# First chunk's turns in a row, two modulation slots moved, and the last expert by column halves with GpSimd adding the others' sum

## The chip, the cores and the metric

The kernel runs on one core of a Trainium2 chip. The metric is device time in microseconds (us). TensorE (PE) has a row of matmuls and one of weight loads (PEld) in the profile; VectorE is DVE, ScalarE is ACT, GpSimd is POOL, SyncE is SP. Line numbers (L447) are those of the kernel before.

## The reference

`reference` runs 256 tokens of width 1024 through two blocks of two layers each, all in float32. Block 1: a gMLP layer (`gelu(rmsnorm(h) @ w_in)`, its second half normed and mixed over 128 tokens by `w_s`, times the first half, `@ w_out`), a gated MLP with a causal convolution of width 3 (`conv_ffn`, hidden 2816), then keys and values, chunked attention with a relative bias, and a second `conv_ffn`. Block 2 is steered by a vector `c`: `silu(c) @ ada_w + b` gives shift, scale and gate for each half layer. Its even layer has forgetting and sliding window attention and a gated MLP, its odd layer sparse attention and a mixture of 8 experts, two for each token:

```
for e in experts:            # tokens that chose e
    y_e = (silu(x @ w_gate[e]) * (x @ w_up[e])) @ w_down[e]
x = x + gate * sum_e(weight_e * y_e)
out = rms_norm(x, final_norm)
```

## The kernel before

**Weights as a stream.** All weights come in one row of slots of up to 128 x 2048 numbers (1 MB), in the order of use (`Plan`, L101 to 163). SP's `load` (L359) fills a ring of `RAW` = 6 buffers; slot s waits until slot s - 6 is used. For precision each weight slot is split in two: ACT writes `whi`, the rounded part (`split`, L1122), DVE writes `wlo`, the rest (`split`, L1665, its instruction L1677). PE makes three products for each 128 rows (`mm3`, L446: lines L447 to L449), high by high, high by low and low by high. The activations are held as `xhi` and `xlo` (`ahi`, `alo` for hidden values). A weight slot of four 128-row blocks costs PE 24 matmuls of 512 columns where there are two token tiles, 12 where there is one gathered tile (the experts).

**Chunks.** A projection is worked in chunks of 512 columns (`product`, L453): two slots each where the input is 1024 wide, six for 2816 (`down0`, `down1`: the first of the six is half a slot). Below, the slots of one projection are numbered from 0. `gmlp_in` has chunks 0 to 3, chunk 0 in slots of 2, 2 and 4 blocks (`FIRST`).

**Modulation slots.** The weights of `c` (48 slots of 4 x 512 columns, 24 for each layer) stand between the others, behind the slots that `Plan` names with `behind`. DVE multiplies such a slot by `silu(c)` right after its split of the slot before it (`modulate`, L1685: four instructions, L1701 and L1703). After each second one PE sums the columns (`ada_turn`, L655, L663) once it is through the slot in front; DVE takes the sums in (`take_cols`, `ada_cols`) before the next pair.

**Order of the work.** Each engine has its own program, written out by hand, and engines wait for semaphores. DVE splits up to two slots ahead (`AHEAD`), three and more before a change of stage (`LEAD`, `MORE`). In the convolution stage DVE's `convolve` splits the first slots of `down0` between its taps and its product with the gate. `residual_then` (L1909) adds the last two chunks of `down0` to `h`, splits slot 1 of `kv`, and then makes blocks 4 to 7 of the next `xhi` and `xlo` (`tail`, L1759), for which PE's slot 1 of `kv` waits.

**Start.** PE turns (transposes) blocks 0 to 3 of both token tiles of x (L760), then blocks 4, 5 and 6, 7 (`two`, L539) as the two turning banks come free. ACT copies each pair with the norm's gain (`tail`), DVE casts it to `xhi` and takes the rest for `xlo`. ACT then makes the statistics (`stats`: sums of squares, roots), and only after them splits slots 3 and 4; DVE computes the rope's angles (L2084 to L2097) and then splits slots 3 and 4 (`skip`). Three small loads are issued first on ACT's queue (`posi`, `rows`, `cols`), one from POOL (`rw`).

**Experts.** Expert 0, a hardware loop over 6, and the last one. Each has 12 slots for the hidden values (`hidden` 0 to 5, the last pair half as wide) and 6 for the output (`out_of`, slots o0 to o5, o5 a half). `add_expert` adds the scattered output of the expert before to the sum `macc`, left half while `hidden` 0 is done, right half at j = 4. For the last expert DVE also multiplies `macc` by the gate and adds it to `h` (`sum_into_h`, L2441, tile 0 among the splits of o3 and o4, tile 1 behind them all), and its output is gated, split in high and low, scattered by PE (`scatter(gated=True)`) and added to `h` (`add_gated`, L2429), then normed and stored.

Of the kernel before, what the change touches and what calls it, by code (L numbers as in the profile page):

```python
# [26 lines left out]
P = 128  # L27
# [73 lines left out]
class Plan:  # L101
# [89 lines left out]
def build_program(nc, x_in, cols_in, rows_in, vg_in, fg1_in, fg_in, pos_in, ws_in, toep_in, rw_in, stream_in, out):  # L191
# [3 lines left out]
    with ctx:  # L195
# [120 lines left out]

        def trb(b):

            return ps[:, 6 + b, :].rearrange("p (k s) -> p k s", k=2)
# [36 lines left out]
        def _(sp):  # L356
# [49 lines left out]
        def _(g):  # L406
# [20 lines left out]
            g.dma_start(rw[:, :, :], rw_in.rearrange("(k p) e -> p k e", p=P)).then_inc(sem("rw_landed"), 16)  # L427


# [4 lines left out]
            g.memset(bias[0:DH, :, P + DH:S], NEG).then_inc(sem("bias_ready"), 1)  # L434

            g.wait_ge(sem("h_added"), 7 * NT)
            g.dma_start(gates[:, 0, :], fg_in.to_broadcast([P, D])).then_inc(sem("fg_landed"), 16)


        @block.tensor  # L440
        def _(pe):
# [315 lines left out]
            for t in range(NT):  # L757
                pe.wait_ge(sem(f"x_landed{t}"), 16)
                for k in range(4):
                    m = pe.transpose(trb(k // 2)[:, k % 2, t * P:(t + 1) * P], h[:, t, k * P:(k + 1) * P], ident[:, :])  # L760
# [3 lines left out]
            two(h, 2)  # L764
# [4 lines left out]
            product(W, KT, xhi, xlo, at_slot=blocks_ready, mid=lambda j: None if j else two(h, 3), parts=FIRST)  # L769
# [7 lines left out]
            def spatial(j):  # L777
                if j == 0:
# [3 lines left out]
                    pe.wait_ge(sem("ada_taken"), 1)  # L782
# [209 lines left out]
            def scatter(gated=False):  # L992

                T.up("x_y")
                if not gated:
                    pe.wait_ge(sem("y_copied"), T("x_y"))
                for n in range(2):
                    if gated:
                        pe.wait_ge(sem("yg_split"), T.up("x_ys"))
# [34 lines left out]
            def out_of(i, first=False, turn_next=False):  # L1034
# [3 lines left out]
                for j in range(6):  # L1038
# [13 lines left out]
                    m.then_inc(sem("w_used"), 1)  # L1052


            def expert(i, first=False, last=False):
# [14 lines left out]
                out_of(i, first, turn_next=not last)  # L1070
# [10 lines left out]
            for _ in range(6):  # L1081
                pe.matmul(ps[:, 2, 0:P], tri[:, :], ones[:, :], start=True, stop=True)
            scatter(gated=True)
# [4 lines left out]
            with pe.If(most > P):  # L1088
                with pe.Fori(0, NE) as i:
                    T.loop(i, x_acc=6, x_tr=6, x_g=1, x_xt=2, x_y=1, x_a=6, x_s=2, x_gt=1, x_ys=2)  # L1090
                    n = pe.value_load(count[0:1, bass.ds(i, 1)])
                    with pe.If(n > P):
# [10 lines left out]
                        scatter(gated=True)  # L1103
                    with pe.Else():
                        pe.drain()
                        for name, k in (("g_psum", 2), ("g_turned", 2), ("x_tr", 6), ("gt_psum", 1), ("w_used", EXP), ("y_psum", 2)):
# [5 lines left out]
        def _(act):  # L1112
            T = Tally()
            act.dma_start(posi[:, :], pos_in).then_inc(sem("rows_landed"), 16)
            act.dma_start(rows[:, :], rows_in.to_broadcast([P, R_END])).then_inc(sem("rows_landed"), 16)
# [246 lines left out]
            act.activation(st[:, 26:27], ones[:, 0:1], ACT.Identity)  # L1362
            for t in range(NT):
                act.wait_ge(sem(f"x_landed{t}"), 16)
            act.wait_ge(sem("cols_landed"), 16)
            for r in range(2):
                tail(xT_c, cols[:, C_GA:C_GA + KT], rounds=(r,))
                split(r + 1)
            tail(xT_c, cols[:, C_GA:C_GA + KT], rounds=(2,))
            split(3)  # L1370
            tail(xT_c, cols[:, C_GA:C_GA + KT], rounds=(3,))
            stats(h, False)
# [193 lines left out]
            def output(i, first=False, gated=False):  # L1566
                used[0] += 6
                split(used[0] + MORE, i, EXP)
                if not first:
                    act.wait_ge(sem("y_psum"), T.up("x_y", 2))  # L1570
                if gated:
                    for n in range(2):
                        act.wait_ge(sem("yg"), T.up("x_yg"))
                        act.activation(yhi[:, 4 * n:4 * n + 4, :], yg[:, n * W:(n + 1) * W].rearrange("p (k c) -> p k c", c=P), ACT.Copy)\
                            .then_inc(sem("yg_hi"), 1)
# [37 lines left out]
            with act.If(most > P):  # L1613
                with act.Fori(0, NE) as i:
                    T.loop(i, x_tr=6, x_g=2, x_gp=2, x_y=2, x_sg=6, x_gt=1, x_yg=2)
# [14 lines left out]
                    with act.Else():  # L1630
                        act.drain()
                        for name, k in (("xt_copied", 2), ("xg", 2), ("hi_done", EXP), ("x_silu", 6), ("gt_copied", 1), ("x_hi", 6), ("yg_hi", 2)):
# [17 lines left out]
        def _(dve):  # L1650
# [420 lines left out]

            for r in range(2):
                tail(xT_c, (r,))
                split(r + 1)
            tail(xT_c, (2,))
            split(3)
            tail(xT_c, (3,))
            moments()
            inverses()
            dve.wait_ge(sem("cols_landed"), 16)  # L2080
# [22 lines left out]
            skip(1, slots=len(FIRST))  # L2103
# [7 lines left out]
            take_cols(1)  # L2111
# [297 lines left out]
            def gate_output(i):  # L2409

                dve.wait_ge(sem("w_used"), i * EXP + used[0])
                for n in range(2):
                    c = slice(n * W, (n + 1) * W)
                    dve.tensor_tensor(yg[:, c], ps[:, 3 + n, :], gates[:, 1, c], ALU.mult).then_inc(sem("yg"), 1)
                for n in range(2):
                    dve.wait_ge(sem("yg_hi"), T.up("x_yh"))
                    k = slice(4 * n, 4 * n + 4)
                    dve.tensor_tensor(ylo[:, k, :], yg[:, n * W:(n + 1) * W].rearrange("p (k c) -> p k c", c=P),
                                      yhi[:, k, :].bitcast(F32), ALU.subtract).then_inc(sem("yg_split"), 1)
# [9 lines left out]
            def add_gated(i, name):  # L2429

                for n in range(2):
                    dve.wait_ge(sem("y_psum"), T.up("x_y"))
                    for t in range(NT):
                        o = h[:, t, n * W:(n + 1) * W]
# [5 lines left out]

            def sum_into_h(t):  # L2441

                link(dve.tensor_tensor(macc[:, t, :], macc[:, t, :], gates[:, 1, :], ALU.mult))
                link(dve.tensor_tensor(h[:, t, :], macc[:, t, :], h[:, t, :], ALU.add))

# [5 lines left out]
            def expert(i, first=False, last=False):  # L2451
# [17 lines left out]
                if last:  # L2469
                    sum_into_h(0)  # L2470
# [6 lines left out]
                if last:  # L2477
                    sum_into_h(1)
                    gate_output(i)
# [12 lines left out]
            assert pos[0] == used[0] == QAT["more"]  # L2492

            most = dve.value_load(count[0:1, NE:NE + 1])
            with dve.If(most > P):
                at_last = T("x_y")
                add_gated(slice(NE - 1, NE), "y_added")
                with dve.Fori(0, NE) as i:
                    T.loop(i, x_xg=2, x_silu=6, x_hi=6, x_a=6, x_y=2, x_yh=2, dve=2, xg_ready=2)
# [15 lines left out]
                    with dve.Else():  # L2515
                        dve.drain()
                        for name, k in (("places", 1), ("dve", 2), ("xg_ready", 2), ("g_taken", 1), ("lo_done", EXP), ("x_tok", 6),
                                        ("x_a", 6), ("x_tr_free", 6), ("yg", 2), ("yg_split", 2), ("y_added", 1)):
# [119 lines left out]
```

## Time and profile before

| | us |
|---|---|
| median of 3 runs | 1508.49 (1505.85 to 1509.45) |
| profiled execution, its own time | 1511.99 |
| its span, first to last instruction | 1510.2 |
| PE busy | 1443.1 |
| DVE busy | 1220.9 |
| ACT busy | 899.4 |
| POOL busy | 5.6 |

The span lies 1.8 us below the profiled execution's own time. Busy time of PE contains overlap: matmuls are pipelined, and the start of one to the start of the next is what a matmul costs. A row of the timeline has the start in us, the length in us, engine, line, operation, output <- input, shape and count; in brackets stands the idle time of the engine before it and what ended it. Rows of one kind that follow each other are merged (x2).

### The profile page before, as it was taken

The page shows a single profiled execution, that of the slowest core. Times are in us where ns is not written, and L with a number is a line of the kernel's source. Part 1 is how long each engine was busy: PE and PEld are TensorE (multiplying, and loading weights), DVE is VectorE, ACT ScalarE, POOL GpSimd, SP SyncE. Part 2 cuts the span into 40 slices and gives each one's busy share as a digit, 9 for nine tenths or more (in the row PEclk, how much of TensorE's full clock was granted, in tenths as well). Part 3 has the DMA queues.
Part 4 walks back from the last instruction along what each step waited for, and adds up shares of the span by engine and source line. Part 5 has one row for each costly group of instructions (what it writes and reads, how often), then busy time and mean ns, then how long its engine had stood idle before and what let it go on. Part 6 is the DMA issues. An engine that isn't in the chain of part 4 may idle for free.

```text
span 1510.2 us, 19548 instructions
## 1 busy us (share of the span) xinstructions
PE 1443.1 (96%) x7128; PEld 1185.2 (78%) x7129; DVE 1220.9 (81%) x1664; ACT 899.4 (60%) x1207; POOL 5.6 (0%) x18
## 2 busy tenths in 40 slices
PE   6999999999999999998999999979899999999996
PEld 5888888887788887886788887856687888888885
DVE  6776879767767889878878788696688989999997
ACT  6555664556666563567433334446676877787764
POOL 0000000000000000000000000000000000000000
PEclk9999999999999999999999999979899999999999
DMA  8565446875355458561566786422289899898983
GB/s 295 230 227 191 167 169 235 336 265 221 112 205 186 154 181 305 212 240 59 205 262 256 268 311 231 167 84 85 112 326 343 317 330 325 341 355 328 335 325 138
DMA packets 53422, 356.15 MB, mean 236 GB/s; under 512 B 6096, under 2 KB 7120, under 8 KB 12896
## 3 DMA queue, kind: packets, MB, share of 16 engines
q1 hardware_dynamic: 52592, 352.15, 62.7%
q0 software_dynamic: 320, 2.65, 0.5%
q8 instruction: 49, 0.80, 0.2%
q10 hardware_dynamic: 432, 0.30, 0.1%
q14 instruction: 29, 0.24, 0.1%
HBM read 354.03 MB, written 1.05 MB: 235 GB/s over the span
## 4 chain that ended last, share of the span: by engine, by line
PE 76%; DVE 14%; ACT 5%; DMA 3%; issue 2%; SPq 0%; DVEq 0%; ACTq 0%
PE ps L447 23%; PE ps L449 22%; PE ps L448 22%; DVE wlo L1677 4%; DMA raw<-stream_dram 3%; PE ps L612 1%; ACT whi L1133 1%; DVE acc L1703 1%; PE ps L539 1%; PE ps L663 1%; PE ps L688 1%; DVE tok L1928 1%; ACT attn_scratch L1319 1%; PE ps L717 1%; DVE xlo L1767 1%
## 5 line engine op out<-in xcount | busy, mean ns | idle before, releaser
L1677 DVE TENSOR_TENSOR wlo<-raw,whi 128x2048 fp32r<-128x2048 f32 (+2 forms) x302 | 645.5, 2163 | 91.9 <-ACT whi L1133 78.4
L1133 ACT ACTIVATE whi<-raw 128x2048 fp32r<-128x2048 f32 (+2 forms) x302 | 541.8, 1817 | 183.1 <-DMA raw<-stream_dram 177.8
L447 PE MATMUL ps<-whi,xhi 128*128 128x512 f32 (+3 forms) x1360 | 534.0, 393 | 13.5 <-DVE xlo L2382 4.2
L449 PE MATMUL ps<-whi,xlo 128*128 128x512 f32 (+3 forms) x1360 | 522.6, 384 | 0.0
L448 PE MATMUL ps<-wlo,xhi 128*128 128x512 f32 (+3 forms) x1360 | 521.8, 384 | 0.0
L447 PEld LDWEIGHTS ps<-whi,xhi 128*128 128x128 f32 x1360 | 257.1, 189 | 70.2 <-issue 8.5
L449 PEld LDWEIGHTS ps<-whi,xlo 128*128 128x128 f32 x1360 | 256.9, 189 | 51.6
L448 PEld LDWEIGHTS ps<-wlo,xhi 128*128 128x128 f32 x1360 | 257.5, 189 | 46.7
L447 PE MATMUL ps<-whi,ahi 128*128 128x512 f32 x440 | 174.7, 397 | 3.7 <-DVE wlo L1677 2.5
L449 PE MATMUL ps<-whi,alo 128*128 128x512 f32 x440 | 171.7, 390 | 0.0
L448 PE MATMUL ps<-wlo,ahi 128*128 128x512 f32 x440 | 171.3, 389 | 0.0
L1703 DVE SCALAR_TENSOR_TENSOR acc<-raw,cs,acc 128x512 f32<-128x512 f32 x168 | 126.1, 751 | 5.1
L1928 DVE SCALAR_TENSOR_TENSOR tok<-ps,cols,tok 128x255 f32<-128x255 f32 (+1 forms) x176 | 72.7, 475 | 41.1 <-ACT tok L1283 40.3
L447 PEld LDWEIGHTS ps<-whi,ahi 128*128 128x128 f32 x440 | 82.6, 188 | 23.2 <-issue 4.1
L449 PEld LDWEIGHTS ps<-whi,alo 128*128 128x128 f32 x440 | 82.6, 188 | 17.7
L448 PEld LDWEIGHTS ps<-wlo,ahi 128*128 128x128 f32 x440 | 82.7, 188 | 16.3
L1187 ACT ACTIVATE tok<-ps,st 128x512 f32<-128x512 f32 x64 | 40.5, 685 | 55.1 <-PE ps L612 35.8
L1288 ACT ACTIVATE tok<-tok 128x512 f32<-128x512 f32 x22 | 13.9, 632 | 65.6 <-DVE tok L1928 65.6
L1283 ACT ACTIVATE tok<-ps,cols 128x256 f32<-128x256 f32 x88 | 42.5, 576 | 3.8 <-DVEq L1946 3.8
L1552 ACT ACTIVATE tok<-ps 128x256 f32<-128x256 f32 (+1 forms) x48 | 17.3, 360 | 42.4 <-PE ps L449 42.2
L1319 ACT ACTIVATE attn_scratch<-attn_scratch,sx 128x128 f32<-128x128 f32 x80 | 35.3, 445 | 10.0 <-DVE sx L2009 9.9
L1303 ACT ACTIVATE tok<-ps 128x512 f32<-128x512 f32 x11 | 6.6, 598 | 52.9 <-PE ps L449 52.9
(316 smaller groups left out, 1164.9 us busy)
## 6 DMA issues: line engine op xcount, KB each, us to landing
raw<-stream_dram SPq DMA_DIRECT2D x315, 1024.0 KB, 4.9
raw<-stream_dram SPq DMA_DIRECT2D x32, 512.0 KB, 4.7
attn_scratch<-toep_dram POOLq DMA_DIRECT2D x1, 2048.0 KB, 11.8
raw<-stream_dram SPq DMA_DIRECT2D x2, 528.0 KB, 4.4
h<-x_dram SPq DMA_DIRECT2D x2, 512.0 KB, 4.7
y<-tok SPq DMA_DIRECT2D x4, 256.0 KB, 2.6
head_scratch<-w_s_dram SPq DMA_DIRECT2D x1, 512.0 KB, 14.4
head_scratch<-vg_dram SPq DMA_DIRECT2D x1, 512.0 KB, 11.5
```

What stands on the lines that cost most here:

```text
L447: pe.matmul(o, xh, wh, start=start, stop=False)
L448: pe.matmul(o, xh, wl, start=False, stop=False)
L449: return pe.matmul(o, xl, wh, start=False, stop=stop)
L539: last = pe.transpose(trb(n % 2)[0:src.shape[1], k - r, t * P:(t + 1) * P], src, ident[:, :])
L1133: act.activation(whi[:, q % SPL, 0:w], raw[:, s % RAW, 0:w], ACT.Copy).then_inc(sem("hi_done"), 1)
L1187: m = act.activation(dst[:, t], src[:, t], func, scale=st[:, 6 + t:7 + t])
L1283: m = act.activation(conv[:, f, :], ps[:, 6 + f // 2, (f % 2) * S:(f % 2 + 1) * S], ACT.Identity, scale=sc, bias=bi)
L1319: m = act.activation(x, x, ACT.Exp, bias=neg_max(u, t), scale=-1.0, accum_out=total(u, t))
L1552: act.activation(sgx[:, 0:m], ps[:, (2, 0, 1)[j % 3], m:2 * m], ACT.Silu).then_inc(sem("x_silu"), 1)
L1677: dve.tensor_tensor(low(q)[:, 0:w], raw[:, s % RAW, 0:w], whi[:, q % SPL, 0:w].bitcast(F32), ALU.subtract).then_inc(sem("lo_done"), 1)
L1703: m = dve.scalar_tensor_tensor(acc[:, :], wk, cs[:, kk:kk + 1], acc[:, :], ALU.mult, ALU.add)
L1928: m = dve.scalar_tensor_tensor(o, src, cols[:, c:c + 1], o, ALU.mult, ALU.add)
```

## The change

1. `gmlp_in` has no modulation slots any more; `down0` gets one behind its slot 2 and `kv` one behind its slot 1.
2. PE turns all eight blocks of x in a row into four banks (`first_of`), followed by four matmuls that nobody reads. ACT writes `xhi` out of the banks (`first_high`), DVE `xlo` (`first_low`).
3. ACT splits slot 3 between squares and roots and slots 4 and 5 behind them; DVE splits slots 3, 4 and 5 ahead of the angles.
4. `cols` is loaded first; `posi` and `rows` are issued by ACT once `x` and `cols` have landed; `w_s` is issued behind slot 3, `vg` behind slot 6, `rw` behind the bias load at the second layer.
5. `out_of` of the last expert works o3 to o5 by column halves: the left half of all three, then the right half. The left half is gated and split while PE works on the right one and scattered ahead of o5's right part (`scatter_left`); the right half is scattered unsplit, as float32 (`scatter_right`). The six matmuls in front of the scatter (L1082) are gone.
6. POOL does `sum_into_h`, by column halves, each half as soon as `add_expert` has finished it; DVE waits for it ahead of `add_gated`.

```diff
-        proj("gmlp_in", 2 * D, G_ORDER, layer=0, behind=(4, 5), first=FIRST)
+        proj("gmlp_in", 2 * D, G_ORDER, first=FIRST)
-        proj("down0", D, kt=FK, layer=0, behind=(4, 5, 7, 8, 10, 11))
-        proj("kv", 2 * D, layer=0, behind=(2, 3, 5, 7))
+        proj("down0", D, kt=FK, layer=0, behind=(2, 4, 5, 7, 8, 10, 11))
+        proj("kv", 2 * D, layer=0, behind=(1, 2, 3, 5, 7))
...
+        def first_of(r):
+            return ps[:, (6, 7, 4, 5)[r], :].rearrange("p (k s) -> p k s", k=2)
...
-                if s == 2:
+                if s == 3:
                     sp.dma_start(ws, ...)
-                if s == 3:
+                if s == 6:
                     sp.dma_start(vg, ...)
...
+            for n, added in enumerate(("y_left", "y_added")):
+                c = slice(n * W, (n + 1) * W)
+                g.wait_ge(sem(added), NE - 1)
+                g.tensor_tensor(macc[:, :, c], macc[:, :, c], gates[:, 1, c]..., ALU.mult).then_inc(sem("h_summed"), 1)
+                g.wait_ge(sem("h_summed"), 2 * n + 1)
+                g.tensor_tensor(h[:, :, c], macc[:, :, c], h[:, :, c], ALU.add).then_inc(sem("h_summed"), 1)
...
-                for k in range(4):
-                    m = pe.transpose(trb(k // 2)[:, k % 2, ...], h[:, t, ...], ident[:, :])
+                for k in range(KT):
+                    m = pe.transpose(first_of(k // 2)[:, k % 2, ...], h[:, t, ...], ident[:, :])
-            two(h, 2)
+            for _ in range(4):
+                pe.matmul(ps[:, 2, 0:S], ident[:, :], h[:, 1, 0:S], start=True, stop=True)
...
+            def scatter_left():
+                pe.wait_ge(sem("yg_split"), T.up("x_ys"))
+                for t in range(NT):
+                    pe.matmul(ps[:, 5 + 2 * t, :], GT[:, t, :], yhi[:, 0:4, :], start=True, stop=False)
+                    pe.matmul(ps[:, 5 + 2 * t, :], GT[:, t, :], ylo[:, 0:4, :], start=False, stop=True)...
+            def scatter_right():
+                pe.wait_ge(sem("yg"), 2 * T("x_ys"))
+                for t in range(NT):
+                    pe.matmul(ps[:, 3 + t, :], GT[:, t, :].bitcast(F32), yg[:, W:D], ...)...
...
+                for n in range(2 if by_half < 6 else 0):
+                    for j in range(by_half, 6):
+                        ...
+                        elif j == 5:
+                            scatter_left()
+                        ...
+                    if n == 0:
+                        m.then_inc(sem("y_half"), 1)
...
+            def first_high(r):
+                act.wait_ge(sem("tr"), T.up("tr"))
+                for j in range(2):
+                    k = 2 * r + j
+                    m = act.activation(xhi[:, k, :], first_of(r)[:, j, :], ACT.Identity, scale=cols[...])
+            for r in range(2):
+                first_high(r)
                 split(r + 1)
+            for r in range(2, 4):
+                first_high(r)
             split(3)
-            stats(h, False)
+            act.activation(st[:, 26:27], ones[:, 0:1], ACT.Sqrt)
+            squares(h, False)
+            split(4)
+            roots()
+            split(6)
...
             moments()
+            split(4)
             inverses()
+            skip(1, slots=len(FIRST))
+            split(6)
...
-                    sum_into_h(0)
...
-                    sum_into_h(1)
-                    gate_output(i)
+                    gate_output(i, by_half=True)
...
+            dve.wait_ge(sem("h_summed"), 4)
```

## Rows read from the trace of the kernel before

**Rows 1.** The page: busy time by engine, and the chain's shares by engine.

```profile
PE 1443.1 (96%) x7128; PEld 1185.2 (78%) x7129; DVE 1220.9 (81%) x1664; ACT 899.4 (60%) x1207; POOL 5.6 (0%) x18
...
PE 76%; DVE 14%; ACT 5%; DMA 3%; issue 2%; SPq 0%; DVEq 0%; ACTq 0%
```

**Rows 2.** Timeline of the start, 12 to 53 us: PE, ACT and DVE.

```profile
13.45 0.63 PE L448 MATMUL ps<-wlo,xhi 128*128 128x512 f32 x1
...
13.88 0.63 PE L449 MATMUL ps<-whi,xlo 128*128 128x512 f32 x1
...
16.19 1.91 ACT L1133 ACTIVATE whi<-raw 128x2048 fp32r<-128x2048 f32 x1 [0.80 <-DMA raw<-stream_dram]
...
18.14 2.29 DVE L1677 TENSOR_TENSOR wlo<-raw,whi 128x2048 fp32r<-128x2048 f32 x1 [1.15 <-ACT whi L1133]
...
29.75 0.50 PE L447 MATMUL ps<-whi,xhi 128*128 128x512 f32 x1 [1.60 <-DVE wlo L1677]
...
40.97 1.27 ACT L1187 ACTIVATE tok<-ps,st 128x512 f32<-128x512 f32 x2 [3.59 <-PE ps L449]
...
46.21 0.95 PE L663 MATMUL ps<-ones,acc 128*128 128x1 f32 x8
...
50.46 4.49 DVE L1677 TENSOR_TENSOR wlo<-raw,whi 128x2048 fp32r<-128x2048 f32 x2
...
58.45 3.61 PE L784 MATMUL ps<-tok,head_scratch 128*128 128x256 f32 x16
```

**Rows 3.** Stretches: us, busy time and count of each engine, PEclk, DMA share, GB/s.

```profile
30.00:41.00 11.00, 11.00 (x50) 9.07 (x50) 10.48 (x12) 6.83 (x7) 0.00 (x0) 1.00 0.43 162
...
1081.00:1085.00 4.00, 4.00 (x10) 3.13 (x11) 3.41 (x4) 3.23 (x2) 0.00 (x0) 0.50 0.00 0
```

**Rows 4.** Timeline of DVE and PE at the start of `down0`.

```profile
231.11 2.29 DVE L1677 TENSOR_TENSOR wlo<-raw,whi 128x2048 fp32r<-128x2048 f32 x1
...
243.82 2.33 DVE L1703 SCALAR_TENSOR_TENSOR acc<-raw,cs,acc 128x512 f32<-128x512 f32 x3
...
248.32 2.29 DVE L1677 TENSOR_TENSOR wlo<-raw,whi 128x2048 fp32r<-128x2048 f32 x1
...
250.76 0.47 PE L447 MATMUL ps<-whi,ahi 128*128 128x512 f32 x1 [0.62 <-DVE wlo L1677]
```

**Rows 5.** Timeline of DVE and PE at the start of `kv`.

```profile
290.07 2.29 DVE L1677 TENSOR_TENSOR wlo<-raw,whi 128x2048 fp32r<-128x2048 f32 x1
...
295.81 0.69 DVE L1767 TENSOR_TENSOR xlo<-tok,xhi 128x512 fp32r<-128x512 f32 x1
...
296.55 0.50 PE L447 MATMUL ps<-whi,xhi 128*128 128x512 f32 x1
```

**Rows 6.** Timeline of the last expert: DVE and PE.

```profile
1456.52 2.29 DVE L1677 TENSOR_TENSOR wlo<-raw,whi 128x2048 fp32r<-128x2048 f32 x1 [0.19 <-ACT whi L1133]
...
1462.44 0.48 PE L447 MATMUL ps<-whi,xhi 128*128 128x512 f32 x1
...
1479.15 4.48 DVE L1677 TENSOR_TENSOR wlo<-raw,whi 128x2048 fp32r<-128x2048 f32 x2
...
1486.52 1.22 DVE L2443 TENSOR_TENSOR tok<-tok,gates 128x1024 f32<-128x1024 f32 x1
...
1489.03 2.29 DVE L1677 TENSOR_TENSOR wlo<-raw,whi 128x2048 fp32r<-128x2048 f32 x1
...
1491.47 0.47 PE L447 MATMUL ps<-whi,ahi 128*128 128x512 f32 x1 [0.88 <-DVE wlo L1677]
...
1495.91 1.29 DVE L2414 TENSOR_TENSOR tok<-ps,gates 128x512 f32<-128x512 f32 x2 [0.63 <-PE ps L449]
...
1499.36 2.73 DVE L2435 SCALAR_TENSOR_TENSOR h<-ps,comb,h 128x512 f32<-128x512 f32 x4 [0.70 <-PE ps L1003]
```

**Rows 7.** Timeline of POOL and DVE at 302 us.

```profile
301.58 2.33 DVE L1703 SCALAR_TENSOR_TENSOR acc<-raw,cs,acc 128x512 f32<-128x512 f32 x3
...
302.07 0.95 POOL L434 MEMSET attn_scratch<- 64x1024 f32 x1 [11.29 <-DMA attn_scratch<-toep_dram]
```

More of the change, by code:

```diff
@@ L763, in _ @@
                         T.up("tr")
-            two(h, 2)
+            for _ in range(4):
+                pe.matmul(ps[:, 2, 0:S], ident[:, :], h[:, 1, 0:S], start=True, stop=True)
             def blocks_ready(j, k):
                 pe.wait_ge(sem("x_ready"), T.up("x_ready", FIRST[j] // 2))
-            product(W, KT, xhi, xlo, at_slot=blocks_ready, mid=lambda j: None if j else two(h, 3), parts=FIRST)
+            product(W, KT, xhi, xlo, at_slot=blocks_ready, parts=FIRST)
             pe.wait_ge(sem("ws_landed"), 16)
@@ L1032, in turn, with out_of @@
                 T.up("x_tr")
-            def out_of(i, first=False, turn_next=False):
+            def out_of(i, first=False, turn_next=False, by_half=6):
                 if not first:
                     pe.wait_ge(sem("y_added"), T("x_y"))
-                for j in range(6):
+                for j in range(by_half):
                     if j == 1 and turn_next:
@@ L1069, in expert @@
                     gather()
-                out_of(i, first, turn_next=not last)
+                out_of(i, first, turn_next=not last, by_half=3 if last else 6)
             gather()
@@ L1080, in _ @@
             expert(0, last=True)
-            for _ in range(6):
-                pe.matmul(ps[:, 2, 0:P], tri[:, :], ones[:, :], start=True, stop=True)
-            scatter(gated=True)
+            scatter_right()
             pe.wait_ge(sem("counted"), 1)
@@ L1102, in _ @@
                         out_of(i)
-                        scatter(gated=True)
+                        scatter_left()
+                        scatter_right()
                     with pe.Else():
                         pe.drain()
-                        for name, k in (("g_psum", 2), ("g_turned", 2), ("x_tr", 6), ("gt_psum", 1), ("w_used", EXP), ("y_psum", 2)):
+                        for name, k in (("g_psum", 2), ("g_turned", 2), ("x_tr", 6), ("gt_psum", 1), ("w_used", EXP), ("y_psum", 2 * NT)):
                             pe.sem_inc(sem(name), k)
@@ L1361, in _ @@
             act.wait_ge(sem("pool"), 5)
-            act.activation(st[:, 26:27], ones[:, 0:1], ACT.Identity)
+            act.activation(st[:, 31:32], ones[:, 0:1], ACT.Identity)
             for t in range(NT):
@@ L1568, in output @@
                 split(used[0] + MORE, i, EXP)
-                if not first:
+                if not first and not gated:
                     act.wait_ge(sem("y_psum"), T.up("x_y", 2))
                 if gated:
[L1572 to L1575, printed above, removed]
+                    act.wait_ge(sem("yg"), T.up("x_yg", 2) - 1)
+                    act.activation(yhi[:, 0:4, :], yg[:, 0:W].rearrange("p (k c) -> p k c", c=P), ACT.Copy).then_inc(sem("yg_hi"), 1)
                 else:
@@ L2070, in _, with first_low @@
                 dve.sem_inc(sem(name), 1)
+            def first_low(r):
+                dve.wait_ge(sem("x_high"), r + 1)
+                for j in range(2):
+                    k = 2 * r + j
+                    m = dve.scalar_tensor_tensor(xlo[:, k, :], first_of(r)[:, j, :], cols[:, C_GA + k:C_GA + k + 1],
+                                                 xhi[:, k, :].bitcast(F32), ALU.mult, ALU.subtract)
+                m.then_inc(sem("x_ready"), 1)
+            dve.wait_ge(sem("cols_landed"), 16)
             for r in range(2):
-                tail(xT_c, (r,))
+                first_low(r)
                 split(r + 1)
-            tail(xT_c, (2,))
+            for r in range(2, 4):
+                first_low(r)
             split(3)
-            tail(xT_c, (3,))
+            T.up("tr", 4)
+            dve.wait_ge(sem("x_ready"), 4)
+            dve.sem_inc(sem("tr_free"), 4)
             moments()
+            split(4)
             inverses()
-            dve.wait_ge(sem("cols_landed"), 16)
+            skip(1, slots=len(FIRST))
+            split(6)
             dve.wait_ge(sem("rows_landed"), 16 * 2)
@@ L2102, in _ @@
             link(dve.tensor_scalar(experts[:, :], iota[:, 0:NE], -1.0, None, ALU.add))
-            skip(1, slots=len(FIRST))
             dve.wait_ge(sem("wsT_ready"), 1)
@@ L2407, in lo_of_output, with gate_output @@
                     .then_inc(sem("y_copied"), 1)
-            def gate_output(i):
-                dve.wait_ge(sem("w_used"), i * EXP + used[0])
+            def gate_output(i, by_half=False):
                 for n in range(2):
+                    if by_half and n == 0:
+                        dve.wait_ge(sem("y_half"), 1)
+                    else:
+                        dve.wait_ge(sem("w_used"), i * EXP + used[0])
                     c = slice(n * W, (n + 1) * W)
                     dve.tensor_tensor(yg[:, c], ps[:, 3 + n, :], gates[:, 1, c], ALU.mult).then_inc(sem("yg"), 1)
[L2415 to L2419, printed above, removed]
+                    if n == 0:
+                        dve.wait_ge(sem("yg_hi"), T.up("x_yh"))
+                        dve.tensor_tensor(ylo[:, 0:4, :], yg[:, c].rearrange("p (k c) -> p k c", c=P), yhi[:, 0:4, :].bitcast(F32),
+                                          ALU.subtract).then_inc(sem("yg_split"), 1)
             def add_expert(i, n):
```

55 lines of the change are left out of this document (32 added, 23 removed).

## The prediction

> **What bounds the kernel now.** The page comes first: PE is busy for 96% of the span, DVE for 81%, ACT for 60%, POOL for nothing, and the chain that ended last runs through PE for 76% of it [rows 1]. The reader is to see a program that is a row of matmuls: what makes PE wait counts in full, what happens beside it counts nothing. So I looked for idle time in front of PE's rows in three stretches: the start, the two places that get a modulation slot, and the last expert. A weight slot costs PE 24 matmuls, 5.45 us (0.227 each; 50 records in 11 us [rows 3]) and DVE 2.2.
>
> **Start (parts 2, 3 and 4).** Before, PE waits 1.60 us for slot 3, because both engines split it late: ACT behind the statistics, DVE behind the angles; its matmuls start at 29.75 [rows 2]. What must come before is slot 2: its DMA lands and ACT starts at 16.19, DVE ends the split at 20.4 [rows 2]. Now nothing else holds PE there (the last turned blocks used to), so slot 2 is worked from 20.5 to 26.0, the turns of `w_s` take until 26.9. ACT: table and squares from 18.1 to 21.7, slot 3 until 23.6; DVE splits it until 25.9, hidden under slot 2. Slot 3 thus starts at 26.9 instead of 29.75: **-2.9**. Slots 4 and 5 follow on DVE until 30.7, ahead of PE's 32.3; the angles end near 35, before the sines need them (39).
> The loads: `cols` is issued 0.9 us earlier, but ACT issues two more before its first copy (about 0.45 each), which cancels. Moving `rw`, `posi` and `rows` away leaves slot 2 at 16.2 or up to 0.7 earlier. `w_s` and `vg` come later and are needed at 26 and 43. So -2.0 to -3.6, if PE's clock holds (below).
> The removed column sums at 46.21 [rows 2] (0.8 from start to start) bring nothing: from PE's end of slot 4 (40.9) a chain of ACT and DVE (the copy at 40.97, statistics, norm, then the split at 50.46 [rows 2]) runs until 52.75, 11.9 us, which PE's slots 5 and 6 (10.9) no longer quite cover.
>
> **Two modulation slots moved (part 1).** The four instructions take 3.0 us (243.31 to 246.29; the second to fourth are the row at 243.82 [rows 4]). DVE did not hurt for them at 32 and 38 us; where they go it does.
> `down0`: behind the split of slot 2 at 231.11 DVE works without a gap through the gate product, slot 3, the taps, slot 4, its modulation, the next product and the split of slot 5 at 248.32, for which PE already waits 0.62 us at 250.76 [rows 4]. The new 3.0 us go in front of all this: PE starts slot 5 at 253.8, **+3.0**. The added slot's DMA, one ring place earlier than slot 3's, has long landed.
> `kv`: DVE splits slot 1 at 290.07 and then makes the last blocks of x, ready at 296.50; PE starts slot 1 at 296.55 [rows 5]. In between DVE idles 1.8 us for ACT. The modulation stands exactly there (292.3 to 295.3); the rest follows, x is ready at 297.9: **+1.3**. And the column sums (0.8) that stood in front of `kv`, beside this chain, now stand behind its slot 1, in the open: **+0.8**. Those behind `down0`'s slot 4 fall into the new idle time; all later ones keep their place.
> Sum **+5.1**. If DVE's queue has slack that I don't see, it is +1 at least (the sums in the open); if ACT or a landing is late too, +6.
>
> **Last expert (parts 5 and 6).** Off DVE go two instructions of 2.5 us together (1486.52 to 1489.03), after which slot o4's split ends late and PE waits 0.88 us at 1491.47 [rows 6]. Without them, and with GpSimd costing nothing: o4 is split by 1488.8, o5 by 1490.2. PE ends o2 at 1487.7, the left halves of o3 to o5 take 15 matmuls, 3.4 us, to 1491.1, each just in time for its split. DVE gates the left half (0.7), ACT and DVE split it (1.3), ready at 1493.4; PE works right halves of o3 and o4 until 1493.8, scatters left (4 matmuls, 0.9), ends o5 at 1495.4, as now. Then DVE gates right (0.7, until 1496.3); PE scatters it as float32: 256 columns cost 0.45 by L784 (3.61 for 8) [rows 2], so two of 512 cost 1.8, to 1498.2; DVE adds the left half meanwhile and ends the fourth addition at 1499.6, where it now ends 2.73 behind 1499.36, at 1502.1 [rows 6]. Norm and store follow as before: **-2.5** (-2.1 to -2.7).
> What GpSimd costs: four instructions with two inputs of 1024 numbers. No row shows such a one. Length: a memset of 1024 took 0.95 [rows 7]; with two reads in turn I estimate 1.9 (bounds 0.95 and 2.4, twice DVE's 1.22 for the same work [rows 6]). Effect on DVE: nothing at the low end; the memset at 302.07 lay over DVE instructions with two inputs and these took 0.75 as always [rows 7]. But it reads nothing. At the high end each holds up DVE's split, which reads two operands itself, for its whole length. I take the high end, since the one row for the low end lacks the reads in question. The first pair comes at 1454, where DVE is 3.7 us ahead (split begun 1456.52, its matmuls at 1462.44 [rows 6]): +0.2. The second comes at 1479.15, right among o1 to o5, which have no slack: one between o1 and o2 moves PE's o2 by 1.2 us, the next pushes o3 to 1489.8, o4 to 1492.1, o5 to 1493.5, and PE ends at 1498.6 instead of 1495.4. That is +3.1 with the first pair's share rounded in. Term: **+3.1**, bounds 0 and 4.3 (length 2.4, first pair 0.7).
> The Trainium skill (SBUF — State Buffer, "SBUF: two separate sides") says that a DVE instruction with two SBUF inputs and a GpSimd one that reads SBUF exclude each other for a whole instruction. No row here shows it; by it the term would be the high end. The Trainium skill (GPSIMD Engine Reference, "Performance versus the Vector engine") gives 4497 ns for such an addition of 2048 numbers; half of it, by estimate 2.25, would make the term 3.9.
>
> **Sum.** -2.9 + 5.1 - 2.5 + 3.1 = +2.8. Against the profiled execution (1511.99, 1.8 of it outside the span) that is 1514.8; against the median, 3.5 lower than that execution, **1511.3**. About 0.3%, 4.5 us, is what a measurement tells from no change: I forecast no change that can be told, a little on the slow side.
>
> **Rivals.**
> 1. GpSimd is free beside DVE: the term of 3.1 goes, -0.3 in all, 1508.2. For it: the memset. Against it: four read streams at once, never seen here.
> 2. Faster: GpSimd is free and the middle costs little, because DVE's order before slot 5 has room (ACT's copies or the taps shrink with it) and only one of the two places counts: -2.9 + 1.3 + 0.8 - 2.5 = -3.3, with slot 2 landing early (-0.7) and the sums hidden (-0.8) -4.8, 1503.7. Against it: DVE's rows from 231 to 250 leave no gap.
> 3. Slower, PE's clock: the first matmuls run at the low level, one each 0.43 us (13.45, 13.88 [rows 2]) instead of 0.227; PE had been busy in pieces. After the idle 4.2 us at 1081 the granted clock is again 0.50, that is 1.2 of 2.4 GHz [rows 3]. The new start leaves PE idle from about 18.7 to 20.5 in front of slot 2. If the clock falls there, 20 of its matmuls cost 0.2 more each, +4.0: 1515.3. It decides from some 12 slow matmuls on. Against it: the four added matmuls and eight turns in a row keep PE busy from 4.8 to 12, so the clock should rise earlier than now; an idle 1.60 at 29.75 did not lower it (the page's mean stays 393 ns).
>
> **How the numbers follow.** Forecast case 0.42 (own range 1509.5 to 1513.5), rival 1 0.29, rival 2 0.14, rival 3 0.15. Range 1503.5 to 1516: from the low ends (-3.6 + 2 - 2.7 + 0) to the high ends (-2 + 6 - 2.1 + 4.3), a little cut at the top. Faster than 1504: over half of rival 2 and a tail of rival 1, 0.12. Slower than 1513: most of rival 3 and a quarter of the forecast case, 0.25. Same 0.63.
>
> **What would show each step.** Start: slot 3's first matmul near 27 without idle time before it, all at 0.23 a matmul from slot 2 on. Middle: PE waits 1 to 3 us twice among slots 3 to 5 of `down0` for L1677, and over 1 us for the last blocks of x at `kv`; the distance from slot 3 of `gmlp_in` to slot 2 of `kv` grows by 5. End: the last addition comes 2.5 us earlier counted from o0's first matmul if the splits of o2 to o5 start as now; if exclusion holds, they start one GpSimd length late. I am wrong if GpSimd's rows overlap unslowed splits (rival 1), if DVE has a gap between 231 and 250 (rival 2), or if slot 2's matmuls are 0.43 apart (rival 3).

## The result, and the profile after

| | us | runs | against the kernel before |
|---|---|---|---|
| changed kernel, first measurement | 1513.12 | 10 | 1.0042 (1.0027 to 1.0056) |
| changed kernel, measured again | 1511.93 | 12 | 1.0019 (1.0003 to 1.0034) |
| kernel before, against itself | 1506.80 | 12 | 0.9978 (0.9961 to 0.9995) |

The change makes the kernel slower, by 6.1 us in the first measurement (medians 1513.12 and 1507.03) and by 3.2 in the second. The last line says how far to trust such a ratio: the kernel before, set against 23 other runs of itself, comes out at 0.9978, that is 3.3 us too low (its two medians, 1506.80 and 1508.70, are 1.9 us apart), and the interval leaves one out. The forecast was 2.8 us more, called no change that can be told, a little on the slow side. The first measurement is above the 0.3% that bounds that, the second below.

The changed kernel's profiled execution took 1515.3 us, its span is 1513.3. Its page, as in [rows 1]:

```profile
PE 1444.0 (95%) x7124; PEld 1183.8 (78%) x7125; DVE 1220.6 (81%) x1659; ACT 898.9 (59%) x1206; POOL 25.3 (2%) x22
PE 72%; DVE 16%; ACT 6%; DMA 3%; issue 3%; DVEq 0%; ACTq 0%; SPq 0%
```

PE's work is what it was; POOL has 20 us it did not have, and the share of PE in the last chain falls by 4 points, that of DVE rises by 2. To see where, the traces are laid side by side. The table has the start of ACT's n-th weight split in the changed kernel, less the start of the same split before.

| split begun before at (us) | 23 | 56 | 232 | 264 | 299 | 333 | 627 | 1091 | 1455 | end |
|---|---|---|---|---|---|---|---|---|---|---|
| changed kernel | -5.0 | -6.4 | -6.4 | -3.4 | -0.3 | +0.7 | +1.0 | +1.3 | +3.8 | +3.1 |
| the same, second trace | -5.1 | -6.5 | -6.5 | -3.5 | -0.5 | +2.1 | +2.4 | +2.6 | -0.6 | -0.1 |

So 6.4 us are won at the start, all of them are lost between 232 and 333 us, then little happens until the experts (1091 to 1455), whose length is a matter of the single execution (359.0 to 365.7 us in 14 traces of twelve kernels; 363.1 in the trace of before).

**Start.** PE and ACT of the changed kernel; the rows of before are [rows 2].

```profile
7.82 0.84 ACT L1410 ACTIVATE xhi<-ps,cols 128x256 fp32r<-128x256 f32 x2 [5.07 <-PE ps L769]
...
11.01 0.47 PE L456 MATMUL ps<-whi,xhi 128*128 128x512 f32 x1 [0.46 <-DVE wlo L1726]
11.31 0.39 PE L457 MATMUL ps<-wlo,xhi 128*128 128x512 f32 x1
11.54 0.40 PE L458 MATMUL ps<-whi,xlo 128*128 128x512 f32 x1
...
12.58 1.96 ACT L1169 ACTIVATE whi<-raw 128x2048 fp32r<-128x2048 f32 x1
...
17.01 0.47 PE L456 MATMUL ps<-whi,xhi 128*128 128x512 f32 x1 [0.29 <-DVE wlo L1726]
...
23.37 0.47 PE L456 MATMUL ps<-whi,xhi 128*128 128x512 f32 x1
```

ACT no longer waits for a load before its first copy; it splits slot 2 at 12.58 (16.19 before), and slot 3's first product stands at 23.37, with no idle time before it, where it was 29.75. The products of slot 0 stand 0.23 us apart (11.31, 11.54), where before they stood 0.43 apart until 17.7 (13.45, 13.88 [rows 2]). The first is PE's spacing at 2.4 GHz, the second at 1.2: with all turns and the four added matmuls in a row, its clock has risen before the first product.

**down0 and kv.** The changed kernel, PE and DVE; before, [rows 4] and [rows 5].

```profile
234.45 0.47 PE L456 MATMUL ps<-whi,ahi 128*128 128x512 f32 x1 [1.60 <-DVE wlo L1726]
...
247.40 0.47 PE L456 MATMUL ps<-whi,ahi 128*128 128x512 f32 x1 [0.74 <-DVE wlo L1726]
...
272.78 2.29 DVE L1726 TENSOR_TENSOR wlo<-raw,whi 128x2048 fp32r<-128x2048 f32 x1
278.75 0.95 PE L672 MATMUL ps<-ones,acc 128*128 128x1 f32 x8
279.73 0.16 DVE L1774 TENSOR_TENSOR scl<-ps,cols 128x4 f32<-128x4 f32 x1 [4.67 <-PE ps L672]
280.52 2.33 DVE L1752 SCALAR_TENSOR_TENSOR acc<-raw,cs,acc 128x512 f32<-128x512 f32 x3
283.00 2.29 DVE L1726 TENSOR_TENSOR wlo<-raw,whi 128x2048 fp32r<-128x2048 f32 x1
287.33 1.28 DVE L1835 TENSOR_TENSOR h<-ps,h 128x512 f32<-128x512 f32 x2
287.47 0.50 PE L456 MATMUL ps<-whi,xhi 128*128 128x512 f32 x1 [1.37 <-DVE xlo L1816]
...
296.38 0.50 PE L456 MATMUL ps<-whi,xhi 128*128 128x512 f32 x1 [2.28 <-DVE xlo L1816]
```

At kv PE waits twice, not once. DVE stood 4.67 us for column sums (279.73) just before the work that kv needs.

**Last expert.** POOL, DVE and PE of the changed kernel; before, [rows 6].

```profile
1458.36 6.58 POOL L443 TENSOR_TENSOR tok<-tok,gates 128x1024 f32<-128x1024 f32 x1 [391.56 <-DVE tok L2490]
1465.02 4.34 POOL L446 TENSOR_TENSOR h<-tok,h 128x1024 f32<-128x1024 f32 x1
1482.28 4.39 POOL L443 TENSOR_TENSOR tok<-tok,gates 128x1024 f32<-128x1024 f32 x1 [12.92 <-DVE tok L2490]
1486.74 4.31 POOL L446 TENSOR_TENSOR h<-tok,h 128x1024 f32<-128x1024 f32 x1
...
1462.93 0.41 DVE L2461 TENSOR_TENSOR alo<-ps,ahi 128x256 fp32r<-128x256 f32 x1
1463.48 8.02 DVE L1726 TENSOR_TENSOR wlo<-raw,whi 128x2048 fp32r<-128x2048 f32 x2
...
1482.12 6.69 DVE L1726 TENSOR_TENSOR wlo<-raw,whi 128x2048 fp32r<-128x2048 f32 x2
1489.49 5.91 DVE L1726 TENSOR_TENSOR wlo<-raw,whi 128x2048 fp32r<-128x2048 f32 x2
...
1502.39 0.69 DVE L2479 TENSOR_TENSOR tok<-ps,gates 128x512 f32<-128x512 f32 x1 [2.22 <-PE ps L458]
1503.13 1.99 PE L1012 MATMUL ps<-tok,ahi 128*128 128x512 f32 x4 [0.78 <-DVE tok L2479]
1503.55 2.72 DVE L2499 SCALAR_TENSOR_TENSOR h<-ps,comb,h 128x512 f32<-128x512 f32 x4 [0.47 <-issue]
```

Two splits take 4.48 us together when left alone; here they take 8.02, 6.69 and 5.91, so the first pair of GpSimd's instructions costs DVE 3.5 us and the second 3.6. From the right half's gating to the end of the last addition it is 3.9 us (1502.39 to 1506.27); before, 6.2 (1495.91 to 1502.09).

### The profile page after: what moved, and what is told of

It is laid out like the page before. It is cut to its first block, busy times and chain, and to the rows that moved or that the text cites. A ratio compares the mean times of both kernels' runs of the same rounds, so it can differ in the third digit from the quotient of the medians.

```text
span 1513.3 us, 19534 instructions
## 1 busy us (share of the span) xinstructions
PE 1444.0 (95%) x7124; PEld 1183.8 (78%) x7125; DVE 1220.6 (81%) x1659; ACT 898.9 (59%) x1206; POOL 25.3 (2%) x22
## 4 chain that ended last, share of the span: by engine, by line
PE 72%; DVE 16%; ACT 6%; DMA 3%; issue 3%; DVEq 0%; ACTq 0%; SPq 0%
PE ps L456 22%; PE ps L458 21%; PE ps L457 21%; DVE wlo L1726 5%; DMA raw<-stream_dram 3%; DVE acc L1752 2%; ACT whi L1169 1%; PE ps L621 1%; ACT attn_scratch L1355 1%; PE ps L672 1%; PE ps L548 1%; DVE tok L1977 1%; DVE xlo L1816 1%; ACT tok L1376 1%; DVE tok L1911 1%
## 5 line engine op out<-in xcount | busy, mean ns | idle before, releaser
L1726 DVE TENSOR_TENSOR wlo<-raw,whi 128x2048 fp32r<-128x2048 f32 (+2 forms) x302 | 652.3, 2186 | 89.3 <-ACT whi L1169 73.6
L456 PEld LDWEIGHTS ps<-whi,ahi 128*128 128x128 f32 x440 | 82.6, 188 | 26.9 <-issue 7.4
L457 PEld LDWEIGHTS ps<-wlo,ahi 128*128 128x128 f32 x440 | 82.7, 188 | 16.1
```

The source lines that it names most:

```text
L456: pe.matmul(o, xh, wh, start=start, stop=False)
L457: pe.matmul(o, xh, wl, start=False, stop=False)
L1726: dve.tensor_tensor(low(q)[:, 0:w], raw[:, s % RAW, 0:w], whi[:, q % SPL, 0:w].bitcast(F32), ALU.subtract).then_inc(sem("lo_done"), 1)
```

## The experiments

Each ran in 7 to 12 timed runs, 11 and 12 in one each. A ratio is taken against runs of the kernel before in the same set: their median is 1508.14 for experiments 1 to 4, 1509.18 for 5 to 8 and 1508.70 for 9 to 12, against 1507.03 for the first measurement. Differences of medians between sets thus hold an error of up to 2 us. "Last expert" is the time from the split that before begins at 1454.6 to the end of the span.

**1. The slots back in gmlp_in.**

```diff
-        proj("gmlp_in", 2 * D, G_ORDER, first=FIRST)
+        proj("gmlp_in", 2 * D, G_ORDER, layer=0, behind=(5, 6), first=FIRST)
...
-        proj("down0", D, kt=FK, layer=0, behind=(2, 4, 5, 7, 8, 10, 11))
-        proj("kv", 2 * D, layer=0, behind=(1, 2, 3, 5, 7))
+        proj("down0", D, kt=FK, layer=0, behind=(4, 5, 7, 8, 10, 11))
+        proj("kv", 2 * D, layer=0, behind=(2, 3, 5, 7))
...
-            split(6)
+            split(5)
+            split(6, hold=True)      # slot 5's modulation behind the angles
```

> The changed kernel with its two moved modulation slots back in gmlp_in, now behind its slots 5 and 6 (DVE's idle time at 33 to 40 us), down0 and kv as before. Theory A (the two traces): the early landings gave 6.4 us at the start, the slots took 7.1 away in down0 and kv. Here the modulation delays the norm chain behind 40 us by at most 1.3 us, so the shift against the kernel before is -5.1 to -6.4 at q7 and stays that until the experts: 5.8 us less than the changed kernel, 1507.3, level with the kernel before. Theory B: what is gained ahead of the experts is given back there, because their weights come at the DMA's pace: 1512 to 1513, as the changed kernel, with more idle time of PE in the loop.

1506.22, ratio 0.9988 (0.9974 to 1.0001): 6.9 us below the changed kernel's first median, 5.7 below its second. In the trace the splits are 5.1 to 5.2 us early from 186 us on, and in down0 and kv nothing of that is lost. This is theory A.

**2 and 3. The sum on DVE, at its old places (2) and where DVE waits (3).**

```diff
-            for n, added in enumerate(("y_left", "y_added")):   # POOL's four instructions
...
+                    if last and j == 3:      # 3: left half, product and addition
+                        sum_half(0, 0)
+                        sum_half(0, 1)
...
+                    sum_half(1, 0)           # 3: right half's product, ahead of gate_output
...
+                            sum_half(1, 1)   # 3: its addition, behind the left low part
```

> The changed kernel with the sum into h back on DVE, at the two places where the kernel before has it; the column halves stay. Theory A (GpSimd's four instructions block DVE's splits for 3.4 and 3.6 us): DVE loses 2.5 us instead of 3.6 in front of o4, and 2.5 in front of the left gate product, with 1.1 us of idle time there before: 1 to 2.5 us faster than the changed kernel, 1510.6 to 1512. Theory B (GpSimd costs nothing, the stretched splits only hide idle time): 2.5 to 3.6 us slower than the changed kernel, 1515.6 to 1516.7.

> The changed kernel with the sum on DVE in places where DVE waits anyway: the left half behind hidden 3 (DVE idle 3.6 us there in the kernel before), the right half's product in front of the left gate product (1.1 us idle), its addition behind the left half's low part (2.2 us idle). Theory A: the whole price of GpSimd's blocking goes, 3 to 4 us less than the changed kernel, 1509 to 1510. Theory B (the last expert is bound by landings, not by DVE's splits): less than 1 us.

2: 1511.77, ratio 1.0026 (1.0012 to 1.0040); 3: 1506.98, ratio 1.0004 (0.9990 to 1.0017), which is 6.1 and 4.9 us below the changed kernel's two medians. The last expert lasts 54.1 us in 2 and 52.1 in 3, against 55.65 on average with GpSimd (seven traces, 54.9 to 56.2) and 55.15 in the kernel before's form (four, 53.3 to 56.3). Trace of 3, DVE:

```profile
1467.28 1.23 DVE L2510 TENSOR_TENSOR tok<-tok,gates 128x1024 f32<-128x1024 f32 x1
1468.54 1.22 DVE L2512 TENSOR_TENSOR h<-tok,h 128x1024 f32<-128x1024 f32 x1
...
1475.60 4.48 DVE L1719 TENSOR_TENSOR wlo<-raw,whi 128x2048 fp32r<-128x2048 f32 x2
...
1480.77 4.49 DVE L1719 TENSOR_TENSOR wlo<-raw,whi 128x2048 fp32r<-128x2048 f32 x2
```

Without GpSimd the same splits are 4.48 and 4.49 long, and DVE does the sum's work in 1.2 us a piece. Both times came out inside theory A's numbers or below them. By its time alone, 2 is not told from the changed kernel's second measurement (1511.93); what shows the blocking is the length of the splits and of the last expert.

**4. Both (1 and 3 together).**

> Both: the modulation slots behind slots 5 and 6 of gmlp_in, and the sum on DVE in its idle places. Theory A: the two gains add, 5.8 and 3.5, 1503.8: 3 us faster than the kernel before. Theory B (what comes earlier waits in the experts): 1508 or more.

1501.71, ratio 0.9959 (0.9941 to 0.9976): the lowest median, 6.4 us below the kernel before. In its trace PE is 5.8 us early at 333 us, and the last expert lasts 52.1. It differs from 1 by the place of the sum alone, and is 4.5 us below it; it differs from 3 by the two modulation slots alone, and is 5.3 us below it. These comparisons are within one set of runs.

**5. Part 1 alone** (the two moved slots, on the kernel before).

```diff
-        proj("gmlp_in", 2 * D, G_ORDER, layer=0, behind=(4, 5), first=FIRST)
+        proj("gmlp_in", 2 * D, G_ORDER, first=FIRST)
...
-        proj("down0", D, kt=FK, layer=0, behind=(4, 5, 7, 8, 10, 11))
-        proj("kv", 2 * D, layer=0, behind=(2, 3, 5, 7))
+        proj("down0", D, kt=FK, layer=0, behind=(2, 4, 5, 7, 8, 10, 11))
+        proj("kv", 2 * D, layer=0, behind=(1, 2, 3, 5, 7))
```

> The kernel before with part 1 of the change alone: gmlp_in without modulation slots, one more in down0 and in kv. Theory A (the changed kernel's trace): PE stands 3.0 us more in down0 and 4.0 more at kv, and the removed column sums at 46 us bring 0.8 at most: +6.2 to +7.0 us, the biggest loss of the change. Theory B (the prediction): +5.1. Theory C (the slots cost only where the start brings DVE ahead): under +3.

1515.51, ratio 1.0038 (1.0021 to 1.0054), 5.7 us by the ratio. In the trace the shift is -0.4 at 232 us, +2.7 at 264, +5.6 at 299 and +8.3 at 333: 8.7 us, more than either theory, of which 1.6 come from the clock (below). PE:

```profile
240.45 0.47 PE L447 MATMUL ps<-whi,ahi 128*128 128x512 f32 x1 [1.59 <-DVE wlo L1676]
253.39 0.47 PE L447 MATMUL ps<-whi,ahi 128*128 128x512 f32 x1 [0.74 <-DVE wlo L1676]
...
293.45 0.50 PE L447 MATMUL ps<-whi,xhi 128*128 128x512 f32 x1 [1.36 <-DVE xlo L1766]
302.36 0.50 PE L447 MATMUL ps<-whi,xhi 128*128 128x512 f32 x1 [2.24 <-DVE xlo L1766]
```

These are the same four waits as in the changed kernel, to 0.04 us: they belong to part 1 alone.

**6. Parts 2 to 4 alone** (the start; slots as in 1, the last expert as before).

> The kernel before with parts 2, 3 and 4 alone (eight turns in a row, the new order of splits and loads), its two first modulation slots behind slots 5 and 6 of gmlp_in; the last expert as before. Theory A: the 5.2 us by which PE stayed early with this start in the earlier run come out in the time: -5.2. Theory B (a part of it is lost in the experts, whose weights come at the DMA's pace, so an earlier start only waits there): -1 to -3, with more idle time of PE or ACT in the expert loop.

1504.17, ratio 0.9973 (0.9958 to 0.9989): 4.1 us faster by the ratio. PE is 5.7 us early at 333 us. The interval holds both theories. Its expert loop of 359.3 us is one of the shortest, so nothing is seen to be given back there. But 1.6 us are given back ahead of it: the shift goes from -5.1 at 941 us to -3.5 at 984, where the granted clock is 0.84 (940 to 962 us) and was 0.92 before. The trace of 4 has the same step and the same 0.84; the trace of 1, with the same start, has neither (0.92).

**7. Parts 5 and 6 alone** (the last expert).

> The kernel before with parts 5 and 6 alone: the last expert by column halves, GpSimd adding the sum. Theory A (last expert 54.9 us long in the changed kernel from one split to the end, 55.6 before, 52.0 with the sum in DVE's idle places): -1 to +1. Theory B (the slow side of the change sits here after all): +3 to +5, with the expert loop itself longer, though nothing in it is changed. The prediction had +0.6.

1508.82, ratio 0.9997 (0.9981 to 1.0013): no change, theory A. Here GpSimd's first instruction met an idle DVE:

```profile
1451.21 2.42 POOL L441 TENSOR_TENSOR tok<-tok,gates 128x1024 f32<-128x1024 f32 x1 [385.26 <-DVE tok L2462]
1453.71 4.35 POOL L444 TENSOR_TENSOR h<-tok,h 128x1024 f32<-128x1024 f32 x1
...
1451.43 8.77 DVE L1711 TENSOR_TENSOR wlo<-raw,whi 128x2048 fp32r<-128x2048 f32 x2 [0.31 <-ACT whi L1169]
```

It takes 2.42 us by itself, and DVE's two splits take 8.77, which is 4.29 more than alone.

**8, 11 and 12. The loads of the start** in the old order (8), only `posi` and `rows` ahead of `cols` (11), only `rw` at the start (12).

```diff
+            act.dma_start(posi[:, :], pos_in)                        # 8, 11
+            act.dma_start(rows[:, :], rows_in.to_broadcast([P, R_END]))
             act.dma_start(cols[:, :], cols_in)
...
+            g.dma_start(rw[:, :, :], rw_in.rearrange("(k p) e -> p k e", p=P))   # 8, 12
...
+                if s == 2:                                           # 8: w_s; vg at 3
```

> The changed kernel with the loads issued as before: posi and rows ahead of cols on ACT, rw at the start on POOL, w_s and vg behind slots 2 and 3. Theory A (the load order brought what the prediction left out): the weights land near 9, 13.6, 16.2 and 20.4 us again, slot 3's first product moves from 23.4 to about 27, as predicted for the start, and the time is 3 to 3.6 us more than the changed kernel's. Theory B (the turns in a row and the order of splits brought it): slot 3 below 24.5 and under 1 us more.

> The changed kernel with posi and rows issued ahead of cols on ACT, all other loads as changed. With all loads in the old order slot 3's first product came at 26.6 instead of 23.4 us. Theory A (rows, sent to all 128 partitions, holds up the weights): cols lands near 9 and slots 0 to 3 near the old 9, 13.3, 15.9 and 20.1; slot 3's product near 26. Theory B (it is rw on POOL with its small packets): cols later by 2 us at most, slots 1 to 3 as in the changed kernel, slot 3's product below 24.5.

> The changed kernel with rw issued at the start on POOL again, all other loads as changed. Theory A (rows did it): weights and slot 3's product as in the changed kernel, 23.4 within 0.5 us. Theory B (rw did it): slots 1 to 3 land 3 us later, slot 3's product near 26.5.

8: 1516.96, ratio 1.0048 (1.0030 to 1.0065). 11 and 12: one run each, 1514.06 and 1512.85, read by their traces. First ACT and PE of 8, then PE of 11, then PE of 12:

```profile
9.26 0.84 ACT L1410 ACTIVATE xhi<-ps,cols 128x256 fp32r<-128x256 f32 x2 [5.56 <-DMA cols<-cols_dram]
...
20.32 0.47 PE L456 MATMUL ps<-whi,xhi 128*128 128x512 f32 x1 [1.57 <-DVE wlo L1726]
...
26.67 0.48 PE L456 MATMUL ps<-whi,xhi 128*128 128x512 f32 x1
```

```profile
13.26 0.47 PE L456 MATMUL ps<-whi,xhi 128*128 128x512 f32 x1 [2.09 <-DVE wlo L1726]
13.57 0.57 PE L457 MATMUL ps<-wlo,xhi 128*128 128x512 f32 x1
13.94 0.63 PE L458 MATMUL ps<-whi,xlo 128*128 128x512 f32 x1
14.36 0.63 PE L456 MATMUL ps<-whi,xhi 128*128 128x512 f32 x1
...
26.66 0.48 PE L456 MATMUL ps<-whi,xhi 128*128 128x512 f32 x1
```

```profile
18.15 0.47 PE L456 MATMUL ps<-whi,xhi 128*128 128x512 f32 x1 [0.97 <-DVE wlo L1726]
...
24.48 0.47 PE L456 MATMUL ps<-whi,xhi 128*128 128x512 f32 x1
```

Slot 3's first product comes at 23.37 in the changed kernel, 26.67 in 8, 26.66 in 11 and 24.48 in 12. From issue to landing `cols` takes 4.3 us when it is issued first (landed 5.1) and 7.4 to 8.2 behind the other two (landed 9.1 in 8, 9.9 in 11). The two equal times have different reasons:

- In 8 PE waits 1.57 us at 20.32 for the split of slot 2, which landed at 15.91 instead of 12.36.
- In 11 slot 2 landed at 13.48 and PE waits for nothing behind 13.26. The late `cols` moves the first product by 2.25 us (11.01 to 13.26), and then PE's clock falls: the granted clock is 0.58 between 13 and 17 us (1.00 in the changed kernel), and seven matmuls stand 0.43 apart (13.94, 14.36). That costs about 1.5 us. So the place of `cols` is worth 3.3 us in this one execution and, by an estimate from these rows, 1.8 where the clock stays up.

Slots 1 to 3 landed 1.1 us later in 11. Its theory A named the right loads and the right time for slot 3, but put slots 1 to 3 at their old landings (13.3, 15.9, 20.1), and they landed at 11.0, 13.5 and 16.1: `cols` is held up by 4.8 us, the weights by 1.1. In 12, where `rw` alone is early, they landed 1.3 to 1.4 us later and PE waits 0.97 us for slot 2 at 18.15; slot 3's product comes 1.1 us later, between the two theories (23.4 and 26.5). Together 1.1 and 1.4 us do not make up the 3.55 us by which slot 2 is late in 8; the last us was not taken apart.

For the whole time, 8 against the second trace of the changed kernel (both with the low clock at kv, below) is 3.4 us later at 333 us, inside theory A's 3 to 3.6; the medians are 5.0 and 3.8 us apart.

**9 and 10. The changed kernel and the kernel before, once more.**

> The changed kernel once more. The parts alone measured +5.7 (slots), -4.1 (start) and -0.4 (end); in the traces the shift at the first block's keys is +0.7 and the last expert 0.4 us longer on average. Theory A (its parts add, the first measurement lay high by what the experts vary): +1 to +4 against the kernel before, 1.001 to 1.003, and an expert loop (first split of the experts to the last expert) of 359 to 363 us instead of 365.7. Theory B (the parts together cost more than alone): +6 again, 1.004, and a loop of 364 or more.

> The kernel before once more, as its own comparison: a ratio of 1.000 within 0.0015 by either theory. Its expert loop, 363.1 us in the trace read so far, comes out anywhere from 359 to 365 if the loop's length is a matter of the single execution, and its last expert at 53 to 56 us (55.6 so far).

The ratios are 1.0019 (1.0003 to 1.0034) and 0.9978 (0.9961 to 0.9995). The second missed its expectation by 0.0007: an interval here leaves out what differs from one set of runs to the next. The expert loops last 359.9 and 360.2 us, against 365.7 and 363.1 in the first traces: the length is a matter of the single execution, as theory A had it. The second trace of the changed kernel also has what rival 3 feared, at another place. Windows at kv, first of the trace read above, then of the second one (us, busy time and count of PE, PEld, DVE, ACT, POOL, then PEclk, DMA share, GB/s):

```profile
296.00:304.00 8.00, 7.62 (x40) 6.53 (x41) 3.78 (x7) 5.55 (x6) 1.81 (x2) 1.00 0.70 227
```

```profile
296.00:304.00 8.00, 7.78 (x31) 6.35 (x31) 2.59 (x4) 4.11 (x3) 1.80 (x2) 0.79 0.54 203
```

There are 31 matmuls instead of 40: behind the waits of 1.36 and 2.26 us seven or eight matmuls stand 0.43 us apart, at 1.2 GHz. That costs 1.6 us (between 299 and 333 us the shift grows by 2.6 instead of 1.0).

## Why the prediction was right in sign and off in size

| term | predicted | traces |
|---|---|---|
| start | -2.9 | -6.4 |
| slot in down0 | +3.0 | +3.0 |
| slot in kv | +2.1 | +4.0, and 1.6 more in 5 of 8 traces |
| last expert without GpSimd | -2.5 | -3.1 (52.1 for 55.15) |
| GpSimd | +3.1 | +3.6 (55.65 for 52.1) |
| sum | +2.8 | +1.1, +2.1 with the clock's mean share |

- **Start: the term that was mis-sized.** Two steps on the loads failed. "Moving `rw`, `posi` and `rows` away leaves slot 2 at 16.2 or up to 0.7 earlier" was 3.8 (landed 12.4 for 16.2). "ACT issues two more before its first copy (about 0.45 each), which cancels" counted the issues and not the landing: `cols` landed 4.3 us earlier than before (5.1 for 9.4), since it no longer stands behind `posi` and `rows`. Experiment 8 is the proof that the loads are what was missing: with the old loads the start's new order gives -3.1 at 56 us, the -2.9 that was worked out, and slot 3 at 26.67 for the forecast 26.9. Either early landing alone is not enough: 11 loses 3.3 us of the gain and 12 loses 1.1. Rival 3 (a lower clock in front of slot 2) did not come: the products of slots 2 and 3 are 0.23 apart in every trace. What it feared came in 11, in front of slot 0.
- **down0: right**, -6.4 to -3.4, and the waits came at slots ahead of which DVE's row is full. Rival 2 falls: the 3.0 us came in full, DVE's order had no room.
- **kv: the second step that was mis-sized.** The sentence "all later ones keep their place" is wrong. DVE takes in a pair's sums before the first slot of the next pair. One more slot in down0 turns the pairs round: (4,5), (7,8), (10,11) become (2,4), (5,7), (8,10), and the slot behind 11 is now the first of a pair, which waits for sums that PE makes behind its slot 10. The 4.67 us at 279.73 are that wait; kv's slot 0 and both halves of `h` come late behind it, and PE's 1.37 at 287.47 was in no sum. The trace of before had the hint: in front of the slot behind 10, the first of its pair, DVE waits for the sums of the pair before, only 0.36 us:

```profile
271.86 0.16 DVE L1725 TENSOR_TENSOR scl<-ps,cols 128x4 f32<-128x4 f32 x1 [0.36 <-PE ps L663]
```

- **GpSimd: right.** Each of its instructions takes 2.2 to 2.4 us (the rows of 4.3 to 4.4 hold the 2.2 us of a split before them; 2.42 alone), inside the bounds and above the 1.9 taken. A DVE split that meets one waits until it has ended. Rival 1 (1508.2) falls. The Trainium skill (SBUF — State Buffer, "SBUF: two separate sides") names this exclusion, and the traces agree: splits, with two SBUF operands, wait, while DVE's instructions that read PSUM and one SBUF operand keep their 0.41 us beside GpSimd (1462.93). The estimate of 2.25 from the Trainium skill (GPSIMD Engine Reference, "Performance versus the Vector engine") is nearer to the measured 2.2 to 2.4 than the 1.9 from the memset.
- **The end without GpSimd: right**, -3.1 for -2.5, though the 55.15 is a mean of four traces that lie 3.0 us apart (53.3 to 56.3). The float32 scatter (two matmuls, four records) took 1.99, estimated 1.8.
- **The range** does not follow from the ends that the prediction names: they give -4.3 and +6.2, that is 1504.2 to 1514.7, and the range is wider on both sides, not cut.

The two errors, -3.5 and +1.9 (+2.9 with the clock), have opposite signs and largely cancel; that the sum stands near what was measured is luck. What stays open is the rest: the traces add up to +2.1, the measurements say +6.1 and +3.2. The parts alone (5.7, -4.1, -0.4 by their ratios) give 1.2. Since the ratio of the kernel before to itself is off by 3.3 us, a mean of +4.6 is not told from +2.1. The first interval alone (+4.1 to +8.5 us) would exclude +2.1, the second (+0.5 to +5.1) does not. No part of the traces shows a place for more.

## What to carry to other kernels

A small load whose data the first instruction needs goes first on its queue: behind two others `cols` was issued 0.9 us later and landed 4.0 to 4.8 us later. When two experiments give the same number, read the waits in both before you call it the same cause: 8 and 11 agree to 0.01 us by two different ways. When an item is put into a sequence that is worked in pairs, write down the new pairs and what each waits for, since every later one changes. Work handed to GpSimd beside a DVE that is busy with two SBUF operands isn't free work: find where DVE waits for PE and put it there.

## What the runs showed of the hardware that was not expected

- PE's clock at kv: behind two waits of about 1.36 and 2.26 us it fell in five of eight traces with the same waits (granted 0.79 from 296 to 304 us in the one shown); in the other three it stayed at 1.00. The same code is 1.6 us longer or not by this alone, and the step at 941 to 984 us in 4 and 6 is of the same size.
- PE's clock at the start: behind one wait of 2.09 us it fell in 11 (0.58 from 13 to 17 us), and behind 1.57 us in 8 it did not.
- The record of a GpSimd instruction that has to wait holds its wait too: 6.58 us in a row for 2.2 of work, since two DVE splits ended first.
- The expert loop, unchanged in all kernels, lasted 359.0 to 365.7 us. That spread of 6.7 us is larger than the 6.1 and 3.2 measured between the two kernels, so one trace of it proves nothing.
